# Sliding-window attention in four-head units ordered by a clock per engine, and conditioning pieces kept beside the feed-forward

## The reference

```
c_act = silu(c)
for i in range(4):                                     # layer i = l in the kernel
    sh1, sc1, g1, sh2, sc2, g2 = split(c_act @ ada_w[i] + ada_b[i], 6)
    h = rmsnorm(x, gain[i, 0]) * (1 + sc1) + sh1
    y = (swa, gla, fox)[i % 3](h) @ w_o                # swa for layers 0 and 3
    x = x + g1 * y
    h = rmsnorm(x, gain[i, 1]) * (1 + sc2) + sh2
    x = x + g2 * ((silu(h @ w_g) * (h @ w_u)) @ w_down)    # width 2816
return rmsnorm(x, final_norm)

def swa(h):        # 16 query heads of 64, 4 key/value heads, window 128, blocks of 128
    q, k, v = split(h @ w_in);  q, k = rope(q), rope(k)
    scores = q @ k.T / 8       # block t = 0 sees its own 128 keys, t = 1 sees 256
    scores = where(band, scores, -inf)
    p = softmax(concat([scores, sink], -1))[..., :-1]      # a sink logit for each head
    return p @ v
```

## Time and profile before

| | |
|---|---|
| Median of 3 runs | 2432.14 us (2431.95 to 2434.07) |
| The profiled execution's own time | 2432.57 us |
| Its span | 2430.8 us |
| Busy: PE, DVE, ACT, POOL | 92%, 67%, 43%, 8% of the span |
| Mean granted clock of PE | 0.96 |

### The profile page before, as it was taken

One profiled execution on the slowest core, in us unless ns is written; L12 is line 12 of the kernel. 1 busy time (PEld: TensorE's weight loads), 2 busy tenths in 40 slices (PEclk: granted clock), 3 DMA queues, 4 the chain that ended last, 5 costly groups with the idle time before them and its releaser, 6 DMA issues. The chain is left out here.

```text
span 2430.8 us, 33994 instructions
## 1 busy us (share of the span) xinstructions
PE 2240.5 (92%) x13701; PEld 1972.0 (81%) x13701; DVE 1631.8 (67%) x2343; ACT 1040.4 (43%) x1705; POOL 199.0 (8%) x212
## 2 busy tenths in 40 slices
PE   6999998799999989878999986999999999979997
PEld 5999887689998877766998864899886799857996
DVE  5576677666667677677898665778745654667554
ACT  4444444344544444445333341434433444445432
POOL 1000001000000001110000122001100001110000
PEclk8999999899999999989999998999998999989999
DMA  8866675567677655443999520588631555524561
GB/s 280 286 207 221 219 238 169 184 199 235 214 229 221 219 176 180 164 152 110 314 358 341 200 96 35 173 311 291 224 118 44 165 186 187 185 79 147 174 212 66
DMA packets 305537, 474.68 MB, mean 195 GB/s; under 512 B 20416, under 2 KB 168314, under 8 KB 305380
## 3 DMA queue, kind: packets, MB, share of 16 engines
q1 hardware_dynamic: 295252, 440.68, 54.6%
q0 software_dynamic: 10128, 31.83, 4.4%
HBM read 466.00 MB, written 6.42 MB: 194 GB/s over the span
## 5 line engine op out<-in xcount | busy, mean ns | idle before, releaser
L147 DVE TENSOR_TENSOR wlo<-raw,whi 128x1024 fp32r<-128x1024 f32 x640 | 775.0, 1243 | 237.3 <-ACT whi L141 235.2
L141 ACT ACTIVATE whi<-raw 128x1024 fp32r<-128x1024 f32 x640 | 643.1, 1052 | 150.3 <-DMA raw<-in_ffn_w_gu 77.4
L135 PE MATMUL G<-HTh,whi 128*128 128x256 f32 x2304 | 662.7, 288 | 3.1 <-DVE pool L155 2.1
L135 PE MATMUL G<-HTl,whi 128*128 128x256 f32 x2304 | 653.2, 283 | 0.0
L135 PE MATMUL G<-HTh,wlo 128*128 128x256 f32 x2304 | 653.1, 283 | 0.0
L135 PEld LDWEIGHTS G<-HTh,whi 128*128 128x128 f32 x2304 | 443.2, 192 | 9.4 <-issue 6.2
L135 PEld LDWEIGHTS G<-HTl,whi 128*128 128x128 f32 x2304 | 443.4, 192 | 2.3
L135 PEld LDWEIGHTS G<-HTh,wlo 128*128 128x128 f32 x2304 | 443.0, 192 | 0.0
L141 ACT ACTIVATE pool<-G 128x512 f32<-128x512 f32 (+1 forms) x224 | 122.4, 569 | 618.8 <-PE G L135 562.4
L135 PE MATMUL G<-whi,HTh 128*128 128x512 f32 (+1 forms) x768 | 309.3, 403 | 15.0 <-ACT HTh L141 10.4
L135 PE MATMUL G<-whi,HTl 128*128 128x512 f32 (+1 forms) x768 | 299.5, 390 | 2.1 <-DVE HTl L155 1.5
(11 more groups left out here) (149 smaller groups left out, 2500.7 us busy)
## 6 DMA issues: line engine op xcount, KB each, us to landing
raw<-in_ada_w SPq DMA_DIRECT2D x192, 512.0 KB, 5.7
raw<-in_ffn_w_gu SPq DMA_DIRECT2D x352, 256.0 KB, 5.0
raw<-in_w_in SPq DMA_DIRECT2D x224, 256.0 KB, 4.2
raw<-in_w_in SPq DMA_DIRECT2D x96, 512.0 KB, 4.9
raw<-in_ffn_w_down SPq DMA_DIRECT2D x88, 512.0 KB, 5.5
pool<-mod_rows POOLq DMA_DIRECT2D x24, 512.0 KB, 5.2
raw<-in_swa_w_in SPq DMA_DIRECT2D x24, 512.0 KB, 5.2
raw<-in_gla_w_in SPq DMA_DIRECT2D x24, 512.0 KB, 4.9
```

Source lines behind the costliest of these rows:

```text
L135: return self.e.matmul(out, a, b, start=start, stop=stop, skip_group_check=True) if self.e else self
L141: return self.e.activation(out, a, func, bias=bias, scale=scale, accum_out=accum) if self.e else self
L147: return self.e.tensor_tensor(out, a, b, op) if self.e else self
```

## The change

SWA becomes eight units of four heads, one for each kv head and query block. A unit has nine stages, each on one engine: scores (PE); scale, mask, sink, maximum (DVE); exponentials (ACT); normalisation (DVE); transposes (PE); copy (ACT); values (PE); copy to `OT.hi` (ACT); remainder to `OT.lo` (DVE). All units share accumulator `A0` for the first two stages and `A1` for stages four to eight; `held_up` keeps a unit out while another owns it. There are three seats for `S` and `W`. `advance` writes the stage that can start first by a planned clock for each engine. The queries are projected in steps of one row block (`apart`), keys and queries are transposed for each row block, `tick` takes the place of `step` in `gemm` and in the steps of `Apart`.

In all four layers `out_proj` multiplies the first four blocks of `OT` (`kh = 0`, both columns and both row blocks: eight groups, into all four `G` banks) while SWA's units for kv heads 2 and 3 are still under way, then ends the attention, asks for the gate, scale and shift rows, and does the other eight groups in `turn`. In the turn, both column halves of a row block now come to their residual together; that of block 1, columns 1, and the squares of block 1 are put off until block 0's transposes are split.

`spread` now bars conditioning pieces from the mixers and output projections: 36 stand in the feed-forward of layer 0, 36 in that of layer 1, 24 in that of layer 2 (none in its last 30 pieces).

The diff, cut to its core:

```diff
@@ -361,8 +361,9 @@
         for u in (4, 0, 2, 1, 3, 5):
             add(("fox", l, u), I["fox_w_in_2"][j], D, [(u * 512, 512)])
         wo = I["fox_w_o_2"][j]
-    for u in range(2):
-        add(("wo2", l, u), wo, D, [(u * 512, 512)])
+    for kh in range(2):
+        for u in range(2):
+            add(("wo2", l, u, kh), wo[kh * 512:kh * 512 + 512, :], 512, [(u * 512, 512)])
     for u in range(12):
         if u < 11:
             add(("gu", l, u), I["ffn_w_gu_2"][l], D, [(u * 256, 256), (DFF + u * 256, 256)])
@@ -384,7 +385,7 @@
 def spread(main, extra, skip, end):
 
     ok = [skip <= i < len(main) - end and not any(turning(m[1]) for m in main[max(0, i - 5):i + 2])
-          for i in range(len(main))]
+          and main[i][1][0] not in ("swa", "gla", "fox", "wo2") for i in range(len(main))]
     gave, seen = 0, 0
     res = []
     for i, m in enumerate(main):
@@ -407,8 +408,8 @@
 
     res = spread(layer1_pieces(I, 0) + layer1_pieces(I, 1), ada(0, 1), 12, 24)
     for l in range(4):
-        extra = (ada(2) + ada(3)[:16], ada(3)[16:], [], [])[l]
-        res += spread(layer2_pieces(I, l), extra, (4, 34, 0, 0)[l], 8)
+        extra = (ada(2)[:36], ada(2)[36:] + ada(3)[:24], ada(3)[24:], [])[l]
+        res += spread(layer2_pieces(I, l), extra, 0, (8, 8, 30, 0)[l])
     return res
 
 
...
+    def spend(self, engine, us, ready=0):
+
+        self.clk[engine] = max(self.clk[engine], ready) + us
+        return self.clk[engine]
+
+    def advance(self, done=None):
+
+
+        while done is None or not done():
+            for j in range(len(self.place)):
+                if self.live[j] is None and self.pend:
+                    u = self.live[j] = self.pend.pop(0)
+                    self.age += 1
+                    u["sl"], u["j"], u["age"] = self.place[j], j, self.age
+            can = []
+            for u in self.live:
+                if u is not None and not self.held_up(u):
+                    engine, us = u["stages"][u.s]
+                    can.append((max(u["ready"], self.clk[engine]), u["age"], engine, us, u))
+            if not can or done is None and min(can)[0] > self.clk["PE"]:
+                return
+            at, _, engine, us, u = min(can)
+            self.win(u)
+            u["ready"] = self.spend(engine, us, at) + 0.1
+            u.s += 1
+            if u.s == u.n:
+                self.live[u["j"]] = None
...
+    def held_up(self, u):
+        return u.s in (0, 4) and self.owner[u.s // 4] is not None
+
+    def win(self, u):
+
+
+        i, sl = u.s, u["sl"]
+        if i in (0, 4):
+            self.owner[i // 4] = u
+        elif i == 1:
+            u["nm"], u["su"] = self.smc(4), self.smc(4)
+        elif i == 3:
+            u["rc"] = self.smc(4)
+        self.h_win(u)
+        if i == 1:
+            self.owner[0], self.slots[0].ps_free = None, [u.ev("ve", "s")]
+        elif i == 8:
+            self.owner[1], self.slots[1].ps_free = None, [u.ev("ve", "lo")]
+            self.OT.write(2 * u["kv"], 2, [u.ev("ve", "lo")], (u["t"],))
+            sl.S_free, sl.W_free = [u.ev("pe", "tr")], [u.ev("pe", "pv")]
+            u["st"]["t"].append(u.ev("ve", "lo"))
+            u["st"]["n"][u["kv"] // 2] += 1
...
+        kT = self.mk_blk(4)
+
+        def kv_T(t, ready):
+            g = self.gbank()
+            tr, done = self.new("pe_tr"), self.new("ac_tr")
+            self.h_kvT(g, t, kvb, ready, kT, self.gfree[g], tr, done)
+            self.gfree[g] = [done]
+            kT.tok = kT.tok + [done]
+
+        def ev_kv(t, ps, full):
+            read, done = rope_bank(ps, t, kvb, t * 512, 4, full)
             copied = self.new("ac_ev")
-            self.h_copy(kvb.a[:, g * 512 + 256:g * 512 + 512], ps[:, 256:512], full, kvb.w + [read], copied)
+            self.h_copy(kvb.a[:, t * 512 + 256:t * 512 + 512], ps[:, 256:512], full, kvb.w + [read], copied)
             kvb.tok = kvb.tok + [done, copied]
+            self.soon.append([3, lambda: kv_T(t, done)])
...
+        st = {"t": [], "n": [0, 0]}
+        seat = Seat(self)
+        self.place[:], self.live[:], self.seats = self.slots + [seat], [None] * 3, True
+        self.clk = {"PE": 0, "DVE": 0, "ACT": 0}
+        qTs = []
+        for u in range(2):
+            qt, qT = self.mk_blk(4), self.mk_blk(4)
+            qTs.append(qT)
+
+            def q_T(t, ready, u=u, qt=qt, qT=qT):
                 g = self.gbank()
                 tr, done = self.new("pe_tr"), self.new("ac_tr")
-                self.h_kvT(g, n2, kvb, kT, self.gfree[g], tr, done)
+                at = self.spend("ACT", 0.6, self.spend("PE", 0.45) + 0.1)
+                self.h_qT(g, t, qt, ready, qT, self.gfree[g], tr, done)
                 self.gfree[g] = [done]
-                kT.tok = kT.tok + [done]
-        self.deferred.append(kv_T)
-        st = {"t": []}
-        qTs = []
-        self.halve()
-        self.OT.write(0, 8, [])
-        for u in range(2):
-            qt = self.mk_blk(4)
-
-            def ev_q(g, ps, full, qt=qt):
-                read, done = rope_bank(ps, g, qt, g * 512, 8, full)
-                qt.tok = qt.tok + [done]
+                qT.tok = qT.tok + [done]
+                if t:
+                    qt.release([tr])
+                pe = 0.45 * (t + 1)
+                stages = (("PE", pe), ("DVE", 0.3 + 1.15 * (t + 1)), ("ACT", 1.75 + 0.45 * t), ("DVE", 0.3 + 0.6 * (t + 1)),
+                          ("PE", pe), ("ACT", 0.1 + 0.5 * (t + 1)), ("PE", pe), ("ACT", 0.4), ("DVE", 0.45))
+                for kv in (2 * u, 2 * u + 1):
+                    self.pend.append(Unit("win", 9, ("swa", l, kv, t), kv=kv, t=t, q=qT, tq=done, k=kT, v=kvb, st=st,
+                                          mask=msk, snk=snk, tms=tms, tsk=tsk, stages=stages, ready=at + 0.1))
+
+            def ev_q(t, ps, full, qt=qt, q_T=q_T):
+                self.spend("DVE", 1.5, self.clk["PE"])
+                read, done = rope_bank(ps, t, qt, t * 512, 8, full)
+                self.soon.append([3, lambda: q_T(t, done)])
                 return [read]
-            self.gemm(self.HT, 0, ("swa", l, u), D, "TT", ev_q)
-
-            def q_T(u=u, qt=qt):
-                qT = self.mk_blk(4)
-                for n2 in range(2):
-                    g = self.gbank()
-                    tr, done = self.new("pe_tr"), self.new("ac_tr")
-                    self.h_qT(g, n2, qt, qT, self.gfree[g], tr, done)
-                    self.gfree[g] = [done]
-                    qT.tok = qT.tok + [done]
-                qt.release([tr])
-                qTs.append(qT)
-                for kv in (2 * u, 2 * u + 1):
-                    for t in range(2):
-                        for hp in range(2):
-                            self.pend.append(Unit("swa", 7, ("swa", l, kv, t, hp), kv=kv, hp=hp, t=t, q=qT, k=kT, v=kvb,
-                                                  st=st, ob=2 * kv, mask=msk, snk=snk, tms=tms, tsk=tsk))
-            self.deferred.append(q_T)
-        self.step()
-        self.deferred.pop()()
-        self.ada_sums(0)
-        self.widen(4)
-        self.drain(lambda: not self.busy())
-        self.whole()
-        for b in qTs + [kT, kvb, cb]:
-            b.release(st["t"])
+            q = self.apart(self.HT, ("swa", l, u), ev_q)
+            for t in range(2):
+                for i in range(4):
+                    q(t, i)
+        while self.soon:
+            self.tick()
+        self.advance(lambda: st["n"][0] == 4)
+
+        def end():
+            self.advance(lambda: not self.busy())
+            self.place[:], self.live[:], self.seats = self.slots, [None] * 2, False
+            seat.close()
+            for b in qTs + [kT, kvb, cb]:
+                b.release(st["t"])
+        return end
...
+    def out_proj(self, l, end):
+
+        gs = {(u, t): self.gbank() for t in range(2) for u in range(2)}
+        for g in gs.values():
+            self.gheld[g] = True
+        for u in range(2):
+            for h in range(2):
+                n, lo = self.take(("wo2", l, u, 0))
+                for t in range(2):
+                    done, g = (("pe_first", "pe_w")[t], n), gs[(u, t)]
+                    self.h_mm1(self.OT, 2 * h, n % NSPL, lo, t, g, h == 0, False, self.gfree[g], done)
+                    self.spend("PE", 1.36)
+                    self.tick()
+                self.give(n, done)
+                for b in (2 * h, 2 * h + 1):
+                    self.OT.free[b] = [done]
+        if end:
+            end()
+        gb = self.mod_row(l, 16)
+        N = self.modulated(l, 1)
+        ws = {}
+
+        def part(t, u, h, late=False):
+            def f():
+                if t == 0:
+                    ws[(u, h)] = self.take(("wo2", l, u, 1))
+                n, lo = ws[(u, h)]
+                done, g = (("pe_first", "pe_w")[t], n), gs[(u, t)]
+                self.h_mm1(self.OT, 4 + 2 * h, n % NSPL, lo, t, g, False, h == 1, [], done)
+                if t:
+                    self.give(n, done)
```

(45 more changed lines are left out.)

175 lines of the change are left out of this document (100 added, 75 removed).

## The result

The kernel after takes 2413.51 us (2410.20 to 2422.59, six executions) against 2432.05 us of the kernel before beside it: ratio 0.9934, 95% interval 0.9912 to 0.9956. It is 0.7% faster; the forecast was 2378.0 us in a range of 2352 to 2410, a gain three times as large, and the measured median is just outside.

A forecast was written before the change was run, and what follows sets the result against it. PE, busy 92% of the span, was taken as the bound. Terms -14.2 - 16.3 (attention) - 19.9 (after it) + 7.2 - 1.8 (turns) - 9.1 (conditioning) = -54.1 us from 2432.14 gave 2378.0, range 2352 to 2410.

The forecast's parts named there:

- E = 16 + 8 x 5.7 = 62: SWA layers: attention's end after the first query group, from start plus eight holds; gains 14.2 us (layer 3), 16.3 (layer 0).
- The hold of 5.7: SWA attention: each unit keeps `A1` from its transposes to its remainder for 5.7 us on average, bounds 3.4 and 8.
- The start at 16: SWA attention: the first unit reaches `A1` about 16 us after the first query group.
- The bound from below: SWA attention: its end cannot come before 54 us, PE's 51.3 us of work plus an end of 3.
- The first rival: SWA attention: planned clock errs, units hold `A1` 7 us or more, end at 74 us, total 2402; chance 0.17.
- The second rival: SWA attention: hand-over stays as slow as in the lockstep, hold 11.9 us, end at 111, total 2476; chance 0.05.
- The third: Feed-forward of layer 2: conditioning only moves, DVE overfills there as layer 0's did (11 us), total 2388; chance 0.08.
- fourth: SWA's merged DVE instructions: DVE pays by the element, 0.4 us more at 1028 elements, total 2384; chance 0.05.
- The conditioning: Feed-forwards: moved pieces change layer 0 by -17.1 us, layer 1 by +1.0, layer 2 by +7.0; net -9.1.
- the +1.8 each: Turns of all four layers: block 1's transposes, then `HTl`, come 1.8 us late in each, +7.2 us in all.
- The argument from `OTl` for layer 1 (-1.8): Layer 1's turn: eight groups instead of four cover DVE's splits of `OT`, removing PE's 1.81 us wait before block 0's transposes.
- the fifth case: SWA and turns: overlap works better, hold 4.7 us, attention's end at 54, no stall in turns, total 2355; chance 0.12.

The follow-up runs named there:

- Mask first: Kernel after, with each unit's first DVE stage (mask, row maximum) written right behind its scores while queries are computed: 2404.86 us, ratio 0.9894.
- six ahead: Kernel after, with stages written up to 6 us behind PE's planned time between query matmuls: 2468.17 us, ratio 1.0177.
- the two runs of the parts: Kernel before with only the new placing of conditioning pieces, 2420.34 us; that plus the new output projection behind the old attention, 2421.42 us.
- pieces unpriced: Kernel after, with fetched weight pieces no longer charged to the planned ACT and DVE clocks: 2397.24 us, ratio 0.9870.
- the kernel unpriced with gap: Kernel after without planned charges for fetched weight pieces, and last query transposes written later, behind attention stages (1.36 us charged to PE): 2394.10 us, ratio 0.9873.

## Why the prediction was wrong

**The step that failed** is "E = 16 + 8 x 5.7 = 62", with the gain of 14.2 and 16.3 us drawn from it. The hold of 5.7 in it is right; the start of 16 is not, and the sum has nothing at all between two units. Measured in layer 3: E = 29.7 (start) + 45.5 (eight holds of 5.7) + 11.2 (pauses) = 86.4, 10.2 us longer than the 76.2 of before, where I had it 14.2 shorter. What follows the attention gave its 10 us, and the two cancel: that is where the gain went.

- *The start at 16*, 13.7 us too short. I added up one unit's stages, each "with a wait", with nothing queued in front. In the trace the first scores begin at 12.2 us, where the sum had 8.7 to 9.2, and the mask runs 10 us behind its scores, held by the planned order. I did not ask what the planner would write ahead of it. Mask first shows that it is not the mask alone: freed there, the unit waits 15.6 us ahead of its normalisation (2120.9 to 2136.5), and starts later still.
- *The pauses, put at nothing*, 11.2 us. The sum takes it for granted that the next unit is normalised whenever `A1` comes free. It was not, and removing one charge from the planner took the pauses down to 3.0 us in both layers with the holds unchanged. This part of the cause is shown by a run.
- *The hold of 5.7*, as measured. The prediction names "if the hold of `A1` is not near 5.7 us" as a sign of being wrong. The hold was right to 0.1 us and E was off by 24, so that sign looked at the wrong term. That the mean agrees does not show its parts: single holds lie between 3.8 and 7.5 us.
- *The sum of the terms.* They are not independent, as the table shows: an earlier start came with longer pauses, so their best values cannot be added.
- *The bound from below.* I gave 54 us, from PE's 51.3 and an end of 3. There was a row against it. The stage is 116.9 us before, and my terms made it 94.5; the change removes no matmul, and the same window of the trace of before has PE busy 94.0 us at a clock of 0.90. Even at the 88.8 us of the best order here, a stage of 94.5 leaves 5.7 us of waits, where the kernel with the shortest stage has 16.9. My list for PE was also too short: scores at 0.6 and 0.4 for the two kinds of unit, where four heads measure 1.13 and 0.71 at full clock. I had halved a row that already was one unit's size: 3.4 us over the eight.

**The rest, point by point.** The first rival has the right words ("the planned clock errs") and the right pace, a unit each 7 us, but it puts this down to `A1` being held longer, which it was not, and its E of 74 kept the early start; it had a chance of 0.17, and the range ended a little past it. Its reason, an instruction written early that blocks its queue, was half the story: stages were written too late, and when they were written too early (six ahead) the loss was greater. My argument against it, that "the planned costs are close to the rows", was true and beside the point. That the charge costs 16 us is shown; that it misleads because it falls when a piece is written and not when it runs is my reading of the code. The second rival's outcome, a kernel slower than before, is what the new attention gives under the old placement of pieces (2441.95 us), so the placement saved the result; but its reason, a slow hand-over, is not what that run shows (6.3 us in layer 0, behind a start 16.5 us later). The third and fourth fall: layer 2's feed-forward took 191.6 us (forecast 192), and the merged DVE instructions cost what the rows gave, 1.22 for the maximum of 1028 and 1.23 for the 1024-wide product.

The conditioning was right in each feed-forward and not only in the net. Layer 0's, from 1145.43 to the next turn's transposes at 1339.57, takes 194.1 us (forecast 194.3). Layer 0's feed-forward window, against the earlier trace rows, has PE full:

```profile
1145.40:1302.60 157.20, 156.10 (x1109) 146.80 (x1108) 132.57 (x157) 65.31 (x75) 13.54 (x11) 1.00 0.87 296
```

But I priced the pieces only there. What they do to the SWA stage of layer 0 (13 us in the new attention, some 3 in the old: 118.8 against 115.3 us) was in no term.

The turns: the +1.8 each was right in kind and too large. Block 0's transposes have no wait, where 1 to 2 us were forecast in the SWA layers. Block 1's come 8.3 us behind block 0's, against 7.7 before in layers 0, 2 and 3: 0.6 us, with a wait of 0.7 for a low part of weights. Behind them PE waits 0.85 to 0.88 us for `HTl` in the turns of all four layers, as forecast, where before it did not. That is 1.5 us (in layer 1, where the distance was 8.7 us before, 0.5), less what is gained ahead of block 0's transposes: in layer 3 of the two runs of the parts the turn costs 0.7 us in all (116.0 us in both up to block 1's transposes, 198.0 against 197.3 behind them). The argument from `OTl` for layer 1 (-1.8) cannot be separated from the clock, below. The loads of the rows did not wait for the last `OTl`, 2173.0 us in place of 2203.8, and the first residual starts at 2194.06, 3.3 us after E, right behind the groups that it adds (forecast 5.3, behind the gate row). So the rows were not what it waited for. The range's lower end, "the fifth case, 2352", is a slip: that case was worked out as 2355.

What stays open: why E does not fall below 87 us even in the best order. With pieces unpriced only 3.0 of its 87.1 us are pauses; the rest is the start (38.1) and the holds (46.1), and no order here shortens both. The chain of work that ended last, in the kernel unpriced with gap (start, length, engine, tile and line), passes through query and output groups, low parts of weights on DVE and attention stages in turn:

```profile
2110.28 1.60 PE G L135 x6
2112.51 0.68 DVE pool L147
2113.20 4.47 DVE wlo L147 x3
2117.67 0.67 DVE S L155 x2
...
2155.65 1.13 DVE wlo L147
2157.17 0.66 PE A L138 x4
```

No run isolates one of them.

## What to carry to other kernels

Before a stage is forecast to shrink, subtract from its forecast length the busy time of its fullest engine in the trace: what is left is the idle time that the plan allows, and it should be compared with the idle time that similar interleaved stretches show. A term that is right (here the hold) says nothing about the pauses between its repetitions: give them a term of their own, and ask what has to be ready when a shared buffer comes free. A static planner with right costs can still order badly: one charge lost 16 us here, writing 6 us more eagerly lost 55, so its threshold and its charges are to be tried in both directions on the chip. Background pieces need a price in every stage in which they stand, and the price depends on what the stage does with its waits: the same placement was worth 11 us on one attention and 28 on the other. Before a difference of totals is explained, its stages should be compared, those with unchanged program too.
